# A decoder-style block in fp32 on one core: the even layer's third stream started three rounds later, and latent attention's preparation folded from 22 rounds into 13

## Chip, cores and metric

One core of one Trainium2 chip runs the whole program in one launch. The metric is the device time of that launch in microseconds. The engines are TensorE (PE in the profile, with PEld for its weight loads), VectorE (DVE), ScalarE (ACT), GpSimd (POOL) and SyncE (SP), which only issues loads.

## The reference, cut to what matters

The input is a sequence of 512 tokens by 1024 features in fp32. A first block is followed by a second one of two layers. The change lies in the mixer of the second block's layer 0, the even layer, which joins four heads of differential attention and four heads of latent attention:

```python
proj = h @ w_in                                       # aq, ak, av, cq, ckv, kr
# differential attention, head hd (4 of them), two softmaxes over the same values
p = probs(q1b, k1) - lam * probs(q2b, k2)
o_a = _rms(p @ va, g_sub) * (1.0 - lambda_init)
# latent attention, 4 heads
q = _heads(_rms(cq, g_cq) @ w_uq, MLA_HEADS)          # 256 -> 4 x (128 + 64)
q_nope, q_rope = q[..., :128], _rope(q[..., 128:], pos)
kv = _heads(_rms(ckv, g_ckv) @ w_ukv, MLA_HEADS)      # 128 -> 4 x (128 + 128)
k_nope, vb, k_rope = kv[..., :128], kv[..., 128:], _rope(kr, pos)
sc = (q_nope @ k_nope.T + q_rope @ k_rope.T) * MLA_SCALE
o_b = softmax(where(mask, sc, -inf)) @ vb
return concat([o_a, o_b]) @ w_out
```

## The kernel before

Activations lie as 128 features by 512 tokens. A product with a weight (`dense`, L152 for each matmul) is made in three passes of a split number: the weight's rounded part times the rounded activation, the same times the activation's rest, and the weight's rest times the rounded activation. With 1024 input features that is 8 x 3 = 24 matmuls of 128x512. Each weight unit (128x1024) is loaded into one of four `raw` buffers, rounded by ACT into one of three `wr` buffers (L165, `weight_hi`, two units ahead) and its rest is made by DVE (L171, `weight_lo`, one unit ahead).

`even_layer` weaves three streams. `weave` asks each stream in turn for its next piece of program, up to that stream's next `yield`. One turn of all streams is called a round here. It runs once for each engine with the same rounds, so the order of the instructions on PE, DVE and ACT is fixed when the program is built. Each engine works through its own queue in order, and waits on semaphores count finished instructions of the other engines.

- Stream A holds `mla()`, the preparation of latent attention, then `head(0)` and `head(1)` of latent attention. `mla_tensor`, `mla_vector` and `mla_scalar` write: `kr` (unit 15) with the statistics of two norms, its rotation, units 12 and 13 (`low`, the cq part) with the norm MQ, unit 14 with the norm MK, six products `uq` of 6 matmuls each, two rotations `qrp`, and per head `ukn`, `ukv` (3 matmuls each) and four transposes. On DVE eight multiplications of X by a gain (`scale_vector`, L1530) lie between the `uq`.
- Stream B holds `diff(0)`, `diff(2)` and latent `head(2)`.
- Stream C holds `diff(1)`, `diff(3)` and latent `head(3)`.

`diff` has three products q, k, v of 24 matmuls (one round each), then six steps, then two rounds for its norm (11 rounds). In step i PE makes the scores of query block i (`db_k,db_q` in stream B, `dc_k,dc_q` in C; 128 (i+1) keys, both softmaxes), the products with the values for block i-2, and the transposes of block i-1. DVE normalizes block i-1 (L1604 to L1610) and then finds the maxima of block i (L380). ACT takes the exponentials of block i (L1645) and copies the transposed block i-1 (L1654). In the last step DVE copies the head's output (L1620). A latent head has six rounds of the same kind, with one softmax.

PSUM has 8 banks. Three hold outputs of the streams, and everything else in this layer takes the next of banks 0 to 4 in turn (`K.ring(*range(5))`). PE may write a bank only when its last user has been read, so PE also waits for the exponentials of older scores.

## Time and profile before

| | us |
|---|---|
| median of 3 runs | 2167.02 (2165.88 to 2173.46) |
| profiled execution, its own time | 2172.61 |
| its span | 2171.4 |
| PE busy | 2030.9 (94%) |
| DVE busy | 1088.7 (50%) |
| ACT busy | 873.4 (40%) |
| chain that ended last, share of PE | 85% |

The span is what the trace covers, and lies 1.2 us under that execution's own time. The even layer runs from about 540 us to about 740 us of the span. PE's busy time counts a matmul that runs at the lower clock as busy, so time is lost in two ways: PE idle, and PE busy at half its clock.

### The profile page before, as it was taken

What the parts mean: (1) busy time and instruction counts of PE and PEld (TensorE: products, weight loads), DVE (VectorE), ACT (ScalarE), POOL (GpSimd) and SP (SyncE); (2) the same over time, 40 slices, a digit from 0 to 9 for tenths busy, and PEclk for the clock granted to TensorE, in tenths of its full rate; (3) what the DMA queues carried; (4) which work ended last, traced back from release to release, by engine and by line L of the source; (5) the groups of instructions that cost most, each with busy time, mean ns of one, the idle gap of its engine ahead of it and who ended that gap; (6) DMA issues with size and microseconds to landing.
All of it is one profiled execution on the core that took longest, in us unless ns stands there. A gap on an engine that the chain in (4) does not pass through costs nothing.

```text
span 2171.4 us, 28244 instructions
## 1 busy us (share of the span) xinstructions
PE 2030.9 (94%) x11400; PEld 1613.2 (74%) x11400; DVE 1088.7 (50%) x1929; ACT 873.4 (40%) x1567; POOL 27.3 (1%) x68
## 2 busy tenths in 40 slices
PE   6898888889989999999999999999899999999997
PEld 5765666777766679878888887667478978888886
DVE  5666468737465454354334354444355445343444
ACT  5325443244345444343223243566644344232332
POOL 0000000000000000000000000011000000000000
PEclk9989899999999999999999999999999999999999
DMA  5210011012211123122222222111023212222221
GB/s 200 88 49 21 20 59 49 3 60 101 88 49 49 39 97 127 68 88 97 90 104 89 98 95 88 59 49 49 30 97 113 102 59 97 97 97 97 97 97 69
DMA packets 52050, 169.63 MB, mean 78 GB/s; under 512 B 5776, under 2 KB 9424, under 8 KB 51920
## 3 DMA queue, kind: packets, MB, share of 16 engines
q1 hardware_dynamic: 51920, 167.82, 22.1%
q8 instruction: 92, 1.51, 0.3%
q14 instruction: 38, 0.31, 0.0%
HBM read 165.70 MB, written 2.10 MB: 77 GB/s over the span
## 4 chain that ended last, share of the span: by engine, by line
PE 85%; DVE 9%; ACT 4%; issue 1%; DMA 0%; POOL 0%; SPq 0%; DVEq 0%; ACTq 0%
PE ps L152 83%; PE ps L157 3%; DVE ps L380 1%; DVE wr L171 1%; DVE X L1530 0%; DVE lo L218 0%; DMA cst<-d_cst 0%; DVE macc L233 0%; DVE ra_S L769 0%; DVE rc_S L769 0%; DVE rb_S L769 0%; DVE ra_Z L789 0%; ACT sa_sp L2103 0%; DVE x_acc L233 0%; ACT wr L165 0%
## 5 line engine op out<-in xcount | busy, mean ns | idle before, releaser
L152 PE MATMUL ps<-hi,wr 128*128 128x512 f32 (+1 forms) x4616 | 1406.9, 385 | 50.1 <-DVE wr L171 34.2
L152 PEld LDWEIGHTS ps<-hi,wr 128*128 128x128 f32 x4616 | 861.9, 190 | 230.2 <-DVE wr L171 25.7
L152 PE MATMUL ps<-lo,wr 128*128 128x512 f32 (+1 forms) x2308 | 879.9, 381 | 0.0
L152 PEld LDWEIGHTS ps<-lo,wr 128*128 128x128 f32 x2308 | 439.6, 190 | 84.1 <-issue 3.9
L165 ACT ACTIVATE wr<-raw 128x1024 fp32r<-128x1024 f32 x293 | 307.6, 1052 | 349.6 <-PE ps L152 349.6
L171 DVE TENSOR_TENSOR wr<-raw,wr 128x1024 fp32r<-128x1024 f32 x293 | 356.7, 1217 | 4.3 <-ACT wr L165 2.3
L1457 DVE TENSOR_TENSOR X<-X,ps 128x512 f32<-128x512 f32 x96 | 66.0, 688 | 238.3 <-PE ps L152 238.3
L1986 ACT ACTIVATE mlp<-mlp 128x512 f32<-128x512 f32 x64 | 40.4, 632 | 207.8 <-DVE mlp L1969 207.8
L1969 DVE SCALAR_TENSOR_TENSOR mlp<-ps,R 128x512 f32<-128x512 f32 x64 | 44.3, 692 | 113.2 <-PE ps L152 106.2
L213 ACT ACTIVATE hi<-X,pv 128x512 fp32r<-128x512 f32 x48 | 34.7, 722 | 138.2 <-DVE X L1457 136.2
L1972 DVE TENSOR_TENSOR lo<-mlp,hi 128x512 fp32r<-128x512 f32 x64 | 44.3, 693 | 87.8 <-ACT hi L1990 87.8
L218 DVE SCALAR_TENSOR_TENSOR lo<-X,pv,hi 128x512 fp32r<-128x512 f32 x48 | 36.0, 751 | 40.7 <-ACT hi L213 40.7
L226 ACT ACTIVATE sq<-X 128x512 f32<-128x512 f32 x49 | 30.3, 618 | 28.9 <-DVE X L1457 28.9
L1990 ACT ACTIVATE hi<-mlp 128x512 fp32r<-128x512 f32 x64 | 40.4, 632 | 2.7 <-ACT mlp L1986 0.4
L426 ACT ACTIVATE x_pr<-ps,st 128x256 f32<-128x256 f32 x32 | 15.2, 475 | 61.8 <-DVE st L412 61.8
L233 DVE TENSOR_TENSOR acc<-acc,sq 128x512 f32<-128x512 f32 x50 | 34.6, 693 | 10.0 <-ACT sq L226 5.6
L274 DVE SCALAR_TENSOR_TENSOR Y<-ps,R 128x512 f32<-128x512 f32 x16 | 11.1, 692 | 55.2 <-PE ps L152 47.9
L152 PE MATMUL ps<-x_pt,vt 128*128 128x128 f32 x256 | 34.3, 277 | 2.6 <-ACT x_pt L437 2.6
L152 PEld LDWEIGHTS ps<-x_pt,vt 128*128 128x128 f32 x256 | 32.3, 191 | 5.2 <-ACT x_pt L437 4.3
L152 PE MATMUL ps<-sb_sp,cst 128*128 128x128 f32 (+3 forms) x84 | 26.8, 455 | 7.5 <-POOL sb_sp L2125 7.5
L152 PE MATMUL ps<-sa_sp,cst 128*128 128x128 f32 (+3 forms) x84 | 26.2, 450 | 7.0 <-POOL sa_sp L2125 7.0
L152 PE MATMUL ps<-kt,Y 128*128 128x256 f32 x128 | 32.6, 379 | 0.0
(696 smaller groups left out, 1877.4 us busy)
## 6 DMA issues: line engine op xcount, KB each, us to landing
raw<-d_w SPq DMA_DIRECT2D x128, 512.0 KB, 3.4
raw<-d_wkv SPq DMA_DIRECT2D x32, 512.0 KB, 3.5
raw<-d_w_in SPq DMA_DIRECT2D x30, 512.0 KB, 3.5
raw<-d_sb_w_in SPq DMA_DIRECT2D x24, 512.0 KB, 3.4
raw<-d_ev_w_in SPq DMA_DIRECT2D x16, 512.0 KB, 3.4
raw<-d_wq SPq DMA_DIRECT2D x16, 512.0 KB, 3.5
raw<-d_wo SPq DMA_DIRECT2D x16, 512.0 KB, 3.4
X<-d_xT SPq DMA_DIRECT2D x16, 256.0 KB, 5.1
```

The source lines that it names most:

```text
L152: return pe.matmul(out, lhsT, rhs, start=start, stop=stop, skip_group_check=True)
L157: return pe.transpose(out, in_, M.C("ident")[0:n, 0:n])
L165: a.activation(M.wr[u % 3][:, 0:1024], M.raw[u % 4], ACT.Copy).then_inc(*K.tell("act", "hi", u))
L171: v.tensor_tensor(w[:, 1024:2048], M.raw[u % 4], w[:, 0:1024].bitcast(F32), ALU.subtract).then_inc(*K.tell("dve", "lo", u))
L213: a.activation(hi, src, ACT.Copy, scale=gcol).then_inc(*K.tell("act", *name, "hi", i))
L218: v.scalar_tensor_tensor(out=lo, in0=src, scalar=gcol, in1=hi.bitcast(F32), op0=ALU.mult, op1=ALU.subtract).then_inc(*K.tell("dve", *name, ...
L233: v.tensor_tensor(acc, acc, tmp[i % 2], ALU.add).then_inc(*K.tell("dve", *name, "sum", i))
L1457: v.tensor_tensor(M.X[u], M.X[u], K.bank(*key, u), ALU.add).then_inc(*K.tell("dve", *key, u, frees=(*key, u)))
L1969: v.scalar_tensor_tensor(out=t, in0=K.bank(*key), scalar=0.0, in1=M.R, op0=ALU.max, op1=ALU.mult).then_inc(*K.tell("dve", *key, frees=key))
L1972: v.tensor_tensor(lo[u], t, hi[u].bitcast(F32), ALU.subtract).then_inc(*K.tell("dve", "h", n, q, "lo", u))
L1986: a.activation(t, t, ACT.Square).then_inc(*K.tell("act", *key, "sq"))
L1990: a.activation(hi[u], t, ACT.Copy).then_inc(*K.tell("act", "h", n, q, "hi", u))
```

## The change

The three generators of the preparation merge neighbouring rounds: the rotation of `kr` with units 12 and 13; the statistics of MQ with unit 14; the six `uq` in pairs; both `qrp` rotations in one round; and in the last part the transposes of head h-1 share a round with `ukn` and `ukv` of head h. That makes 13 rounds of 22. Stream C gets `idle(3)` in front. Nothing is computed otherwise. What stands in the rounds (B and C name the step of `diff` or of a latent head):

| round | A before | B, C before | A now | B now | C now |
|---|---|---|---|---|---|
| 1 | kr | q | kr | q | - |
| 2 | kr rotated | k | rotated, 12, 13 | k | - |
| 3 | 12, 13 | v | MQ, 14 | v | - |
| 4 | MQ | step 0 | MK | step 0 | q |
| 5 | 14 | 1 | uq 0, 1 | 1 | k |
| 6 | MK | 2 | uq 2, 3 | 2 | v |
| 7 | uq 0 | 3 | uq 4, 5 | 3 | step 0 |
| 8 | uq 1 | 4 | both qrp | 4 | 1 |
| 9 | uq 2 | 5 | ukv 0 | 5 | 2 |
| 10 to 11 | uq 3, 4 | norm | ukv 1, 2 | norm | 3, 4 |
| 12 to 13 | uq 5, qrp 0 | q, k | ukv 3, end | q, k | 5, norm |
| 14 to 19 | qrp 1, ukv 0, 1, 2 | v, 0 to 4 | head 0 | v, 0 to 4 | norm, q, k, v, 0, 1 |
| 20 to 22 | ukv 2, 3 | 5, norm | head 1 | 5, norm | 2 to 4 |
| 23 to 25 | head 0 | head 2, head 3 | head 1 | head 2 | 5, norm |
| 26 to 28 | head 0 | head 2, head 3 | none | head 2 | head 3 |
| 29 to 31 | head 1 | none | none | none | head 3 |
| 32 to 34 | head 1 | none | none | none | none |

```diff
--- before.py
+++ after.py
@@ -1676,12 +1676,10 @@
     between_tensor(K, M, pe)
     yield
     rope_tensor(K, M, pe, ("kr",), "rot_m", s.kr, K.done("dve", "kr"))
-    yield
     for u in (12, 13):
         dense(K, M, pe, ("low", u), "ev_w_in", u, hi, lo)
     yield
     stats_tensor(K, M, pe, MQ, M.acc, last=1)
-    yield
     dense(K, M, pe, ("low", 14), "ev_w_in", 14, hi, lo)
     yield
     stats_tensor(K, M, pe, MK, M.acc, last=0)
@@ -1694,23 +1692,27 @@
             pe.wait_ge(*K.done("dve", *MQ, "lo", 1))
         unit = dense(K, M, pe, ("uq", m), "uq", m // 4, q_hi, q_lo, nk=2, wk=m % 4 * 2,
                      same=unit if m % 4 else None, last=m in (3, 5))
-        yield
+        if m % 2:
+            yield
     for z in range(2):
         rope_tensor(K, M, pe, ("qrp", z), "rot_m", s.qrp[z], K.done("act", "uq", 4 + z))
-        yield
+    yield
     unit = None
-    for h in range(4):
-        if h == 0:
-            pe.wait_ge(*K.done("dve", *MK, "lo", 0))
-        unit = dense(K, M, pe, ("ukn", h), "ukv", 0, k_hi, k_lo, nk=1, wk=h, same=unit, last=False)
-        dense(K, M, pe, ("ukv", h), "ukv", 0, k_hi, k_lo, nk=1, wk=4 + h, same=unit, last=h == 3)
-        yield
-        b = K.take("ukv", h, "t")
-        pe.wait_ge(*K.clear("ukv", h, "t"))
-        pe.wait_ge(*K.done("act", "ukv", h))
-        for j in range(4):
-            done = tr(pe, M, b[:, j * 128:j * 128 + 128], s.pr[h % 2][:, j * 128:j * 128 + 128])
-        done.then_inc(*K.tell("pe", "ukv", h, "t"))
+    for step in range(5):
+        h = step - 1
+        if h >= 0:
+            b = K.take("ukv", h, "t")
+            pe.wait_ge(*K.clear("ukv", h, "t"))
+            pe.wait_ge(*K.done("act", "ukv", h))
+            for j in range(4):
+                done = tr(pe, M, b[:, j * 128:j * 128 + 128], s.pr[h % 2][:, j * 128:j * 128 + 128])
+            done.then_inc(*K.tell("pe", "ukv", h, "t"))
+        h = step
+        if h < 4:
+            if h == 0:
+                pe.wait_ge(*K.done("dve", *MK, "lo", 0))
+            unit = dense(K, M, pe, ("ukn", h), "ukv", 0, k_hi, k_lo, nk=1, wk=h, same=unit, last=False)
+            dense(K, M, pe, ("ukv", h), "ukv", 0, k_hi, k_lo, nk=1, wk=4 + h, same=unit, last=h == 3)
         yield
 
 
@@ -1731,13 +1733,11 @@
     yield
     v.wait_ge(*K.landed("mcs", 2))
     rope_vector(K, v, ("kr",), s.kr, s.kr, s.cos, s.sin, s.pr[0])
-    yield
     for n, u in enumerate((12, 13)):
         project(K, M, v, ("low", u), s.kn[n])
         add_square(K, v, MQ, n, M.acc, M.sq)
     yield
     low_vector(K, M, v, MQ, 2, "g_cq", s.kn[0:2], M.hi[0][0:2], M.lo[0][0:2])
-    yield
     project(K, M, v, ("low", 14), s.kn[2])
     yield
     low_vector(K, M, v, MK, 1, "g_ckv", s.kn[2:3], M.hi[0][2:3], M.lo[0][2:3])
@@ -1747,14 +1747,13 @@
             weight_lo(K, M, v)
         for i in range(m * ND // 6, (m + 1) * ND // 6):
             scale_vector(K, M, v, FIN, "norm_final_g", i, M.between.R)
-        yield
+        if m % 2:
+            yield
     for z in range(2):
         rope_vector(K, v, ("qrp", z), s.qrp[z], s.qrp[z], s.cos, s.sin, s.pr[z], K.done("act", "uq", 4 + z))
-        yield
-    for h in range(4):
-        if h == 0:
-            weight_lo(K, M, v)
-        yield
+    yield
+    weight_lo(K, M, v)
+    for _ in range(5):
         yield
 
 
@@ -1770,14 +1769,12 @@
     weight_hi(K, M, a)
     factors_scalar(K, M, a)
     yield
-    yield
     for n, u in enumerate((12, 13)):
         weight_hi(K, M, a)
         a.wait_ge(*K.done("dve", "low", u))
         square(K, a, MQ, n, s.kn[n], M.acc, M.sq)
     yield
     low_scalar(K, M, a, MQ, 2, 256, s.kn[0:2], M.hi[0][0:2])
-    yield
     weight_hi(K, M, a)
     a.wait_ge(*K.done("dve", "low", 14))
     square(K, a, MK, 0, s.kn[2], M.acc, M.sq)
@@ -1790,22 +1787,25 @@
         a.wait_ge(*K.done("pe", "uq", m))
         dst = M.Y[4 + m] if m < 4 else s.qrp[m - 4]
         a.activation(dst, K.bank("uq", m), ACT.Copy).then_inc(*K.tell("act", "uq", m, frees=("uq", m)))
-        yield
-    for z in range(2):
-        yield
-    for h in range(4):
-        if h == 0:
-            weight_hi(K, M, a)
-        a.wait_ge(*K.done("pe", "ukn", h))
-        if h == 0:
-            a.wait_ge(*K.done("dve", "qrp", 1, "rope"))
-        a.activation(s.kn[h], K.bank("ukn", h), ACT.Copy).then_inc(*K.tell("act", "ukn", h, frees=("ukn", h)))
-        a.wait_ge(*K.done("pe", "ukv", h))
-        a.activation(s.pr[h % 2], K.bank("ukv", h), ACT.Copy).then_inc(*K.tell("act", "ukv", h, frees=("ukv", h)))
-        yield
-        a.wait_ge(*K.done("pe", "ukv", h, "t"))
-        a.activation(s.vn[h], K.bank("ukv", h, "t"), ACT.Copy).then_inc(
-            *K.tell("act", "ukv", h, "t", frees=("ukv", h, "t")))
+        if m % 2:
+            yield
+    yield
+    for step in range(5):
+        h = step - 1
+        if h >= 0:
+            a.wait_ge(*K.done("pe", "ukv", h, "t"))
+            a.activation(s.vn[h], K.bank("ukv", h, "t"), ACT.Copy).then_inc(
+                *K.tell("act", "ukv", h, "t", frees=("ukv", h, "t")))
+        h = step
+        if h < 4:
+            if h == 0:
+                weight_hi(K, M, a)
+                a.wait_ge(*K.done("dve", "qrp", 1, "rope"))
+            a.wait_ge(*K.done("pe", "ukn", h))
+            a.activation(s.kn[h], K.bank("ukn", h), ACT.Copy).then_inc(*K.tell("act", "ukn", h, frees=("ukn", h)))
+            a.wait_ge(*K.done("pe", "ukv", h))
+            a.activation(s.pr[h % 2], K.bank("ukv", h), ACT.Copy).then_inc(
+                *K.tell("act", "ukv", h, frees=("ukv", h)))
         yield
 
 
@@ -1841,7 +1841,7 @@
 def even_layer(M, mla, head, diff):
     A, B, C = M.even.lanes
     weave(chain(mla(), head(0, A), head(1, A)), chain(diff(0, B), diff(2, B), head(2, B)),
-          chain(diff(1, C), diff(3, C), head(3, C)))
+          chain(idle(3), diff(1, C), diff(3, C), head(3, C)))
```

First place, PE where the scores of the first two differential heads begin (round 4 before). `acc,cst` is the column sum for a norm, `cst,db_pt` the transposes of the values of stream B, `dc` the same of stream C. Before:

```order
L152 MATMUL ps<-acc,cst 128x512
L157 MATMUL ps<-cst,db_pt_312 128x128 x4
L152 MATMUL ps<-db_k,db_q 128x128 x2
L157 MATMUL ps<-cst,dc_pt_320 128x128 x4
L152 MATMUL ps<-dc_k,dc_q 128x128 x2
L152 MATMUL ps<-hi_0_73,wr 128x512
```

In the changed kernel stream C comes to this point three rounds later, in round 7 and 8, with both rotations `mla_qr` behind it:

```order
L157 MATMUL ps<-cst,dc_pt_320 128x128 x4
L152 MATMUL ps<-dc_k,dc_q 128x128 x2
L152 MATMUL ps<-mla_qr_301,cst 128x512
L152 MATMUL ps<-mla_qr_302,cst 128x512
L152 MATMUL ps<-db_pt_311,db_v 128x128 x3
L157 MATMUL ps<-cst,db_pr_310 128x128 x4
L152 MATMUL ps<-dc_k,dc_q 128x256 x2
L157 MATMUL ps<-cst,dc_pr_317 128x128
```

What moved: behind the scores of stream C there is no product of 24 matmuls any more, but the two rotations and the fourth step of stream B.

Second place, DVE at those rotations (L1110, L1111, L1114 are one rotation, L171 a weight's rest, L274 and L277 read a product out of PSUM). Before, in rounds 12 to 14:

```order
L274 SCALAR_TENSOR_TENSOR dc_q<-ps,R 128x512
L1110 TENSOR_TENSOR mla_qr_301<-mla_qr_301,mla_cos 128x512
L1111 TENSOR_TENSOR mla_pr_303<-ps,mla_sin 128x512
L1114 TENSOR_TENSOR mla_qr_301<-mla_qr_301,mla_pr_303 128x512
L171 TENSOR_TENSOR wr<-raw,wr 128x1024
L277 TENSOR_TENSOR db_k<-ps,R 128x512
L171 TENSOR_TENSOR wr<-raw,wr 128x1024
L277 TENSOR_TENSOR dc_k<-ps,R 128x512
L1110 TENSOR_TENSOR mla_qr_302<-mla_qr_302,mla_cos 128x512
```

In the changed kernel, in round 8:

```order
L1110 TENSOR_TENSOR mla_qr_301<-mla_qr_301,mla_cos 128x512
L1111 TENSOR_TENSOR mla_pr_303<-ps,mla_sin 128x512
L1114 TENSOR_TENSOR mla_qr_301<-mla_qr_301,mla_pr_303 128x512
L1110 TENSOR_TENSOR mla_qr_302<-mla_qr_302,mla_cos 128x512
L1111 TENSOR_TENSOR mla_pr_304<-ps,mla_sin 128x512
L1114 TENSOR_TENSOR mla_qr_302<-mla_qr_302,mla_pr_304 128x512
L1604 RECIPROCAL st<-st 128x2
L1606 TENSOR_TENSOR st<-st,omm 128x1
L1607 TENSOR_SCALAR db_pr_310<-db_pr_310,st 128x512
L1610 SCALAR_TENSOR_TENSOR db_pr_310<-db_p_308,st,db_pr_310 128x512
```

What moved: both rotations now stand in one piece, directly ahead of the normalization of stream B's last block.

Third place, DVE in round 20, where a copy of a head's output (L1620, its output `Y_59`) meets the steps of stream C. In the changed kernel:

```order
L380 ISA ps,st<-ps,cmask 128x128
L380 ISA st 128x1
L1620 COPY Y_59<-ps 128x512
L1604 RECIPROCAL st<-st 128x2
L1606 TENSOR_TENSOR st<-st,omm 128x1
L1607 TENSOR_SCALAR dc_pr_318<-dc_pr_318,st 128x256
L1610 SCALAR_TENSOR_TENSOR dc_pr_318<-dc_p_316,st,dc_pr_318 128x256
```

Before, both streams reach this copy in the same round, with nothing of a softmax behind it. What moved: the copy, which waits for the last product of stream B with its values, now stands ahead of the normalization of stream C's block 1.

## Rows read from the trace of the kernel before

**Rows 1.** Stretches of the even layer: start:end, length, busy us (instructions), granted clock

```profile
core 0: us, PE busy (x) PEld busy (x) DVE busy (x) ACT busy (x) POOL busy (x), PEclk, DMA share, GB/s
540.00:588.00 48.00, 47.28 (x203) 37.82 (x202) 21.31 (x26) 12.21 (x15) 0.00 (x0) 1.00 0.28 98
588.00:603.00 15.00, 12.37 (x47) 9.10 (x46) 5.66 (x14) 6.00 (x15) 0.00 (x0) 0.77 0.11 38
603.00:628.00 25.00, 19.49 (x86) 11.16 (x85) 20.39 (x64) 14.38 (x39) 0.00 (x0) 0.86 0.06 22
628.00:671.00 43.00, 43.00 (x191) 34.45 (x190) 21.19 (x27) 13.52 (x18) 0.00 (x0) 1.00 0.25 86
671.00:699.00 28.00, 26.03 (x141) 17.42 (x141) 19.36 (x68) 20.87 (x57) 0.00 (x0) 1.00 0.05 20
699.00:727.00 28.00, 28.00 (x144) 17.46 (x143) 12.99 (x50) 15.03 (x43) 0.00 (x0) 1.00 0.01 1
727.00:739.00 12.00, 9.84 (x47) 5.59 (x46) 4.34 (x16) 4.59 (x14) 0.00 (x0) 1.00 0.00 0
739.00:748.00 9.00, 7.11 (x19) 5.67 (x20) 6.04 (x9) 5.60 (x10) 0.00 (x0) 0.62 0.00 0
```

**Rows 2.** Timeline of PE, 588 to 635 us: start, us, instruction [idle before <-releaser]

```profile
594.03 0.79 PE L152 MATMUL ps<-dc_k,dc_q 64*128 64x128 f32 x2 [2.18 <-ACT db_v L294]
595.27 0.79 PE L152 MATMUL ps<-hi,wr 128*128 128x512 f32 x1 [0.46 <-ACT db_pr L1645]
...
613.48 0.41 PE L157 MATMUL ps<-cst,db_pr 128*128 128x128 f32 x2 [2.64 <-DVE db_pr L1610]
```

**Rows 3.** Timeline of DVE: ends of two dense products, an output's copy, a rotation

```profile
603.36 0.69 DVE L277 TENSOR_TENSOR mla_kn<-ps,R 128x512 f32<-128x512 f32 x1 [6.71 <-PE ps L152]
...
630.04 0.69 DVE L1620 COPY Y<-ps 128x512 f32<-128x512 f32 x1 [1.76 <-PE ps L152]
...
642.24 0.69 DVE L274 SCALAR_TENSOR_TENSOR db_q<-ps,R 128x512 f32<-128x512 f32 x1 [3.23 <-PE ps L152]
...
647.68 0.69 DVE L274 SCALAR_TENSOR_TENSOR dc_q<-ps,R 128x512 f32<-128x512 f32 x1 [3.62 <-PE ps L152]
648.60 0.69 DVE L1110 TENSOR_TENSOR mla_qr<-mla_qr,mla_cos 128x512 f32<-128x512 f32 x1 [0.22 <-PE ps L152]
...
650.53 1.22 DVE L171 TENSOR_TENSOR wr<-raw,wr 128x1024 fp32r<-128x1024 f32 x1
```

**Rows 4.** Timeline of DVE, first instruction of each piece of a differential step

```profile
603.97 0.16 DVE L1604 RECIPROCAL st<-st 128x2 f32<-128x2 f32 x1
...
604.82 0.42 DVE L380 CUSTOM_DVE_ANT_0 ps<-ps,dist 128x256 f32<-128x256 f32 x1
...
617.62 0.74 DVE L1530 SCALAR_TENSOR_TENSOR X<-X,pv,r 128x512 f32<-128x512 f32 x1
618.28 0.16 DVE L1604 RECIPROCAL st<-st 128x2 f32<-128x2 f32 x1
...
619.53 0.69 DVE L380 CUSTOM_DVE_ANT_0 ps<-ps,dist 128x512 f32<-128x512 f32 x1
...
620.78 0.16 DVE L1604 RECIPROCAL st<-st 128x2 f32<-128x2 f32 x1
...
623.97 0.15 DVE L1604 RECIPROCAL st<-st 128x2 f32<-128x2 f32 x1
...
625.42 0.16 DVE L1604 RECIPROCAL st<-st 128x2 f32<-128x2 f32 x1
```

**Rows 5.** Timeline of ACT, one exponential of a 128x512 block

```profile
621.01 0.69 ACT L1645 ACTIVATE db_pr<-ps,st 128x512 f32<-128x512 f32 x1 [1.37 <-DVE st L1604]
```

**Rows 6.** Timeline of PE at the layer's end

```profile
735.59 0.93 PE L152 MATMUL ps<-mla_cos,mla_vn 128*128 128x128 f32 x6 [1.07 <-ACT mla_cos L437]
...
737.71 1.16 PE L152 MATMUL ps<-mla_sin,mla_vn 128*128 128x128 f32 x8 [0.75 <-ACT mla_sin L437]
...
740.89 0.77 PE L152 MATMUL ps<-hi,wr 128*128 128x512 f32 x1 [2.02 <-DVE lo L1438]
```

## The prediction

> **What bounds the kernel now.** The page comes first: PE is busy for 94% of the span and holds 85% of the chain that ended last, so time is lost only where PE waits or where its clock is low. The change touches the even layer alone, so the second view is the table of stretches from 540 to 748 us [rows 1]. The length of a stretch less PE's busy time is idle: 0.72, 2.63, 5.51, 0.00, 1.97, 0.00, 2.16 and 1.89 us, 14.9 us in all. The granted clock has two levels, 2.4 and 1.2 GHz, so a mean of 0.77 over 15 us is 2 x 0.23 x 15 = 6.9 us at the lower one. By the same sum it is 7.0 us between 603 and 628 and 6.8 us between 739 and 748. Everywhere else in the layer the clock is full.
>
> What does the low clock cost? A dense product takes 647.68 - 642.24 = 5.44 us at the full clock [rows 3]. The one that starts at 595.27 [rows 2] is read at 603.36 [rows 3], 8.1 us later, so it cost 2.6 us. Between 603 and 628 PE is busy for 78% of the time, which makes 7.0 x 0.78 / 2 = 2.7 us. After 741 PE is busy throughout: 6.8 / 2 = 3.4 us. Together that is 8.7 us. The whole layer thus loses 14.9 + 8.7 = 23.6 us, 1.1% of the kernel, and this is what a new order of rounds can win at most.
>
> Third view, the timeline of PE, for what it waited for. Before 594.03 stands a wait of 2.18 us until ACT had copied `db_v`, and 0.46 us follow. Before 613.48 stand 2.64 us until DVE had normalized a block [rows 2]. Both lie beside the norms MQ and MK: the chain of a norm goes from PE over ACT and DVE and back over ACT to DVE, and the softmax steps of both streams stand behind it in the same queues. At the end of the layer PE waits 1.07, 0.75 and 2.02 us for the last head's exponential, transposed block and split output [rows 6].
>
> **The change part by part.** PE's work is the same, instruction for instruction. Only idle time and time at the low clock change.
>
> *Rounds 1 to 3.* Only one product stands behind `kr` instead of two, but `kr`'s rotation and unit 12 follow, and the weight's rest for the second product, which PE waited for before (0.72 us [rows 1]), is then covered by the rotation's product. The norm MQ now has unit 14 (5.44 us) over it. Its DVE pieces stand ahead of the rest of stream B's v weight, which I work out to be about 0.4 us late. Idle: 0.4.
>
> *Rounds 4 to 6.* MK and step 0 lie over stream C's q product, and steps 1 and 2 over its k and v: 5.44 us of PE work in each round, where before rounds 4 and 6 had none. The waits of [rows 2] go. What stays are the transposes of blocks 0 and 1, which wait until DVE has done a weight's rest, two or three L1530 and block i-1. An L1530 takes 618.28 - 617.62 = 0.66 us [rows 4]. I count 0.6 + 0.1 us, and 0.4 us for a bank that an ACT copy frees late. Idle: 1.1.
>
> *Rounds 7 to 11* have no dense product. The DVE prices, from start to start, are: block 0 normalized 604.82 - 603.97 = 0.85; block 2 619.53 - 618.28 = 1.25, its maxima of block 3 another 620.78 - 619.53 = 1.25; block 3 625.42 - 623.97 = 1.45 [rows 4]; one rotation 650.53 - 648.60 = 1.93 [rows 3].
> Round 7: PE has two `uq` (12 of the 24 matmuls, 2.7 us), scores of block 3 (1.1 us, an estimate from PE's rate in the same fp32 form) and values (0.5 us), 4.3 us. DVE has reading v (0.6), a weight's rest (1.1), three L1530 (2.0) and block 2 (1.25), 5.0 us. With hand-over times PE waits 0.9 us. Then stream C's second score bank is the one of stream B's block 3, so PE waits for maxima (1.25) and one exponential (0.69 [rows 5]), 1.0 us more than it has work for.
> Round 8: PE has two rotations (1.7 us) and one product with values (0.7 us), then transposes of block 3. DVE must first do two rotations, 3.86 us, and block 3, 1.45 us, and can begin only when PE's first rotation product is done. From there PE has 1.6 us of work against 5.3 us: 3.7 to 3.9 us of waiting, and 0.4 us before it for the bank of the last score. Before, each rotation lay beside dense products, and cost nothing.
> Round 9: a weight's rest, the output copy (0.6 us, after the product with values it waits for) and block 1 stand before stream C's transposes: 1.0 us. Rounds 10 and 11: banks and block 3 of stream C, 1.2 us.
> Sum: 0.9 + 1.0 + 0.4 + 3.9 + 1.0 + 1.2 = 8.4 us idle.
>
> *Rounds 12 to 17* carry six dense products, one each: 0.3 us. *Rounds 18 to 22* have none, and the streams stand three rounds apart: in round 18 stream C's first scores wait for the bank of stream B's block 3 as in round 7 (1.0 us); in 19 and 20 block 3 and the output copy (0.69 us [rows 3], itself waiting for PE) stand ahead of stream C's normalization (0.6 and 0.9 us); with the maxima of head 1, 1.5 us in rounds 21 and 22. Sum 4.0 us, where the same steps idle for 1.97 us before [rows 1]. *Rounds 23 to 28*: 0.3 us.
>
> *Rounds 29 to 31.* Head 3 ends alone, as head 1 does now. Its last three steps have nothing beside them in either kernel. The waits of [rows 6] stay, 3.84 us. Only head 1's first three rounds alone disappear, and they idle for little: 2.16 - 1.07 - 0.75 = 0.34 us.
>
> *Sum of idle.* 0.4 + 1.1 + 8.4 + 0.3 + 4.0 + 0.3 + 3.8 = 18.3 us against 14.9 us: 3.4 us more.
>
> *The clock.* Its first fall before, at 594 us, comes after 2.64 us of idle within six. The wait of round 8 is of that size, so I take one such fall, 2.6 us, in place of the two stretches with 2.6 + 2.7 us. The last fall stays at 3.4 us. That is 2.7 us less. The Trainium skill, "TensorE: Matmul & The Clock Gate", section "A second HAM failure mode: psum-queue depth-cycling", says that PE's short idles between groups of matmuls, as it goes round the PSUM banks, are enough to swing its clock between the two levels. By that rule rounds 7 to 11, which wait on banks and on DVE again and again, would fall more than once, as 603 to 628 does here [rows 1]; the trace agrees in that stretch, and not between 671 and 699, where PE idles 1.97 us in 28 and the clock stays full.
>
> *Net.* +3.4 - 2.7 = +0.7 us on a profiled span of 2171.4 us and its own time of 2172.61 us. That execution is 5.6 us above the median of the runs shown, 2167.02 us, so I carry the difference over: 2167.7, say 2168 us. The work won is real (the norm waits), and it is given back on DVE.
>
> **The rivals.**
> *Faster: the queues slip past each other.* If stream C's three late rounds let DVE run ahead, the hand-made waits of rounds 7 to 11 and 18 to 22 (12.4 us) are half as long, and the clock stays full but for the end. For it: between 699 and 727 us three streams side by side leave PE no idle at all. Against it: there DVE has 13.0 us of work in 28, while rounds 7 to 11 have, by the prices above, about 22 us on DVE against about 20 on PE. Then 6.2 us of idle and the 2.6 us fall go: 2168 - 8.8 = 2159 us.
> *Slower: the pile of round 8 takes the clock down for several rounds.* The place is the transposes of stream B's block 3, behind both rotations. If the clock stays low through rounds 8 to 11, PE's 15 us of work there takes twice as long, less what hides in the waits (about 5 us): +10 us less the 2.6 already counted, about +7.5. The same in rounds 18 to 22, at a third of the size, adds 2: 2177 us. It decides from some 4 us of waiting in one piece on: the largest before, 2.64 us in one piece, was followed by 7 us low at most. By the skill's rule named above this case is the likelier the more banks PE waits for; the rows show it only for 603 to 628.
> *No effect of its own: the losses stay where they are, only with other names*, which is my forecast.
>
> **How the numbers follow.** My case 0.56 (2162 to 2173, from half of the 12.4 us of new waits being off by 5), faster rival 0.23, slower rival 0.21. 0.5% is 10.8 us, about what a measurement of this kernel can tell from no change. Faster than 2156.2 needs the faster rival and 3 us more, also from the end: 0.13. Slower than 2177.9 is the upper half of the slower rival: 0.12. Within: 0.75. The range, 2156 to 2178, reaches over both rivals' centres. The bounds are the 23.6 us that could be won and some 12 us of the slower rival.
>
> **What the profile of the changed kernel would show.** Right: from 588 us on no wait above 1 us for `db_v` or beside the norms; one wait of 3 to 4 us before the transposes of `db_pr`, released by L1610, with L1110 to L1114 twice before it on DVE; waits of 0.5 to 1 us on `dc_pr` near the layer's last quarter; the same three waits at the end, and a low clock behind them. The layer ends within 5 us of 740.9. Wrong: no such wait in round 8 (then DVE was ahead), a clock below 0.7 over 15 us or more, or an end without the fall of the clock.

## The result and the profile after

The changed kernel takes 2173.22 us (median of 20 runs, 2168.98 to 2176.36); the kernel before took 2167.61 us (20 runs, 2164.38 to 2173.52). The ratio is 1.0023, 95% interval 1.0014 to 1.0031: 3.0 to 6.7 us slower, about 5.0. That is clear of noise, and inside the 0.5% that I had called no change. A second series gave 1.0021 [1.0008, 1.0033].

The profiled execution has a span of 2169.1 us and its own time of 2170.41 us, which is *below* before's profiled 2172.61 us. So one pair of executions says the opposite of the medians, and the first thing to read is where two executions of one program differ. I cut each span into three parts: up to the second norm's `facc,cst` product on PE, from there to PE's first product behind the layer, and the rest. The cuts are these rows of PE's timeline (start, us, instruction, [idle before <-releaser]). Before:

```profile
542.68 1.02 PE L152 MATMUL ps<-facc,cst 128*128 128x512 f32 x2
```

The layer's end before is the last of [rows 6]. After, first and last:

```profile
537.54 1.02 PE L152 MATMUL ps<-facc,cst 128*128 128x512 f32 x2
...
733.00 0.94 PE L152 MATMUL ps<-dc_pt,mla_vn 128*128 128x128 f32 x6 [1.07 <-ACT dc_pt L437]
735.12 1.16 PE L152 MATMUL ps<-dc_pt,mla_vn 128*128 128x128 f32 x8 [0.75 <-ACT dc_pt L437]
738.30 0.47 PE L152 MATMUL ps<-hi,wr 128*128 128x512 f32 x1 [2.02 <-DVE lo L1438]
```

The layer is 740.89 - 542.68 = 198.2 us before and 738.30 - 537.54 = 200.8 us after. Cut in the same way, every trace of this study, in us (the last column is the median of that kernel's runs, for the first two kernels of their first series of 20, and the ratio to the kernel before in the same series):

| kernel | ahead | layer | behind | median, ratio |
|---|---|---|---|---|
| before, three traces | 542.7, 538.9, 542.0 | 198.2, 198.3, 198.2 | 1430.5, 1431.1, 1427.4 | 2167.6 |
| changed, three traces | 537.5, 538.1, 542.4 | 200.8, 200.4, 200.6 | 1430.8, 1430.8, 1430.9 | 2173.2, 1.0023 |
| only the packing | 541.6 | 197.7 | 1430.6 | 2168.8, 1.000 |
| scale steps early | 538.4 | 198.0 | 1427.4 | 2168.0, 1.0002 |
| one rotation late | 542.1 | 198.2 | 1430.5 | 2169.9, 1.0007 |
| both rotations late | 536.8 | 194.6 | 1431.0 | 2164.3, 0.9983 |
| rotations late, scales early | 541.7 | 194.5 | 1430.4 | 2165.5, 0.9986 |
| rotations late, no distance | 542.5 | 193.8 | 1430.8 | 2163.9, 0.9983 |
| rotations late, distance 2 | 539.3 | 191.4 | 1427.5 | 2162.2, 0.9968 |
| both moves, distance 2 | 540.7 | 190.5 | 1430.8 | 2161.9, 0.9967 |

The layer repeats within 0.4 us. The parts ahead of it and behind it hold the same instructions in all kernels, and from one execution to the next the first moves by up to 6 us and the second by up to 3.7. So the layer column is read first, and a median of many runs second.

The stretches of [rows 1], in the changed kernel:

```profile
core 0: us, PE busy (x) PEld busy (x) DVE busy (x) ACT busy (x) POOL busy (x), PEclk, DMA share, GB/s
540.00:588.00 48.00, 47.12 (x205) 36.57 (x204) 27.26 (x43) 19.30 (x32) 0.00 (x0) 1.00 0.26 89
588.00:603.00 15.00, 14.91 (x67) 11.51 (x66) 7.56 (x16) 5.96 (x11) 0.00 (x0) 1.00 0.19 69
603.00:628.00 25.00, 18.95 (x76) 11.84 (x75) 16.19 (x46) 9.68 (x28) 0.00 (x0) 0.80 0.12 43
628.00:671.00 43.00, 41.14 (x194) 30.43 (x193) 18.43 (x45) 19.50 (x44) 0.00 (x0) 1.00 0.14 50
671.00:699.00 28.00, 25.62 (x135) 17.96 (x133) 15.88 (x54) 11.22 (x32) 0.00 (x0) 1.00 0.11 38
699.00:727.00 28.00, 25.57 (x128) 15.58 (x128) 14.80 (x50) 15.40 (x45) 0.00 (x0) 1.00 0.00 1
727.00:739.00 12.00, 8.16 (x40) 4.88 (x39) 4.60 (x13) 5.95 (x15) 0.00 (x0) 1.00 0.00 0
739.00:748.00 9.00, 9.00 (x35) 7.28 (x34) 6.08 (x10) 4.67 (x8) 0.00 (x0) 0.81 0.06 18
```

The layer from cut to cut, before and after:

```profile
542.68:740.89 198.21, 183.34 (x842) 131.16 (x840) 104.23 (x263) 88.38 (x201) 0.00 (x0) 0.96 0.15 51
537.54:738.30 200.76, 183.23 (x841) 129.85 (x840) 104.87 (x263) 87.63 (x201) 0.00 (x0) 0.97 0.15 50
```

PE has the same matmuls in both, so a difference in its busy time is read here as what the clock costs, and the rest is idle. Idle time grew from 14.87 to 17.53 us, and busy time is 0.11 us less.

588 to 603 us, which lost 2.63 us of idle and a fall of the clock before, loses nothing now. 603 to 628 idles for 6.05 us in place of 5.51, and has a clock of 0.80: 2 x 0.20 x 25 = 10.0 us at the lower level in place of 7.0. The two stretches from 671 to 727 us idle for 4.8 us in place of 1.97. What sits in 603 to 628 is the pile, on PE and then on DVE:

```profile
606.44 0.52 PE L157 MATMUL ps<-cst,db_pr 128*128 128x128 f32 x3 [0.83 <-DVE db_pr L1610]
...
608.53 0.48 PE L152 MATMUL ps<-dc_k,dc_q 64*128 64x128 f32 x2 [0.72 <-ACT db_pr L1645]
609.20 3.68 PE L152 MATMUL ps<-mla_qr,cst 128*128 128x512 f32 x4 [0.18 <-ACT db_p L1645]
...
617.03 1.09 PE L157 MATMUL ps<-cst,db_pr 128*128 128x128 f32 x4 [3.49 <-DVE st L1604]
...
625.48 0.41 PE L157 MATMUL ps<-cst,dc_pr 128*128 128x128 f32 x2 [0.66 <-DVE dc_pr L1610]
```

```profile
611.26 0.69 DVE L1110 TENSOR_TENSOR mla_qr<-mla_qr,mla_cos 128x512 f32<-128x512 f32 x1 [1.50 <-PE ps L152]
...
613.41 0.69 DVE L1110 TENSOR_TENSOR mla_qr<-mla_qr,mla_cos 128x512 f32<-128x512 f32 x1
...
615.35 0.16 DVE L1604 RECIPROCAL st<-st 128x2 f32<-128x2 f32 x1
...
616.14 0.75 DVE L1610 SCALAR_TENSOR_TENSOR db_pr<-db_p,st,db_pr 128x512 f32<-128x512 f32 x1
```

DVE has waited 1.50 us for PE's first rotation product, does both rotations from 611.26 to 615.35, normalizes block 3, and PE starts its transposes at 617.03, after 3.49 us. (The timeline names `st` L1604 as releaser; L1610 ends at the same moment, 616.14 + 0.75 us.) The transposes then last 1.09 us, where the same four take 0.63 us at the full clock in two kernels below: the clock is at its lower level. The stretches of the same trace, at the places where the clock changed:

```profile
609.34:612.75 3.41, 3.41 (x5) 1.34 (x6) 1.88 (x7) 1.37 (x6) 0.00 (x0) 0.50 0.00 0
612.75:616.17 3.42, 0.79 (x7) 0.60 (x5) 3.18 (x8) 0.00 (x0) 0.00 (x0) 1.00 0.00 0
616.17:622.99 6.82, 5.96 (x20) 4.43 (x21) 3.46 (x10) 3.27 (x9) 0.00 (x0) 0.50 0.09 22
```

It falls twice. The first time is ahead of the wait, for the 3.4 us of the rotation products: the four matmuls take 3.68 us, and 1.98 us at the full clock in a kernel below. The second time begins while PE still waits, at 616.17, and is twice as long. Half of PE's busy time at the low clock is (3.41 + 5.96) / 2 = 4.7 us. That is an estimate of the loss, and a rough one, since the transposes above grew by less than double.

### The profile page after: what moved, and what is told of

It is laid out like the page before. It is cut to its first block, busy times and chain, and to the rows that moved or that the text cites. A ratio compares the mean times of both kernels' runs of the same rounds, so it can differ in the third digit from the quotient of the medians.

```text
span 2169.1 us, 28244 instructions
## 1 busy us (share of the span) xinstructions
PE 2026.7 (93%) x11400; PEld 1608.4 (74%) x11400; DVE 1089.5 (50%) x1929; ACT 873.4 (40%) x1567; POOL 27.4 (1%) x68
## 4 chain that ended last, share of the span: by engine, by line
PE 85%; DVE 10%; ACT 3%; issue 1%; DMA 0%; POOL 0%; SPq 0%; DVEq 0%; ACTq 0%
PE ps L152 82%; PE ps L157 3%; DVE ps L380 1%; DVE wr L171 1%; DVE X L1530 0%; DMA cst<-d_cst 0%; DVE lo L218 0%; DVE macc L233 0%; DVE ra_S L769 0%; DVE rc_S L769 0%; DVE rb_S L769 0%; DVE x_acc L233 0%; DVE nsa_pra L401 0%; ACT sa_sp L2103 0%; ACT L248 0%
## 5 line engine op out<-in xcount | busy, mean ns | idle before, releaser
L171 DVE TENSOR_TENSOR wr<-raw,wr 128x1024 fp32r<-128x1024 f32 x293 | 356.9, 1218 | 4.3 <-ACT wr L165 2.3
L274 DVE SCALAR_TENSOR_TENSOR Y<-ps,R 128x512 f32<-128x512 f32 x16 | 11.1, 692 | 53.3 <-PE ps L152 46.1
```

The costliest lines, as they stand in the source:

```text
L171: v.tensor_tensor(w[:, 1024:2048], M.raw[u % 4], w[:, 0:1024].bitcast(F32), ALU.subtract).then_inc(*K.tell("dve", "lo", u))
```

## The experiments

The theory on trial: the layer loses its time at the pile of round 8, where DVE does two rotations and block 3 with nothing for PE beside them, by the wait and by what it does to the clock. The rivals: the packing itself (any order of the preparation in 13 rounds), the eight L1530 steps of rounds 5 to 7, and the distance of three rounds. In the expectations these are the pile theory and, for the distance, the stagger theory. Every kernel below computes the whole reference.

**Only the packing.** The distance is taken out of the changed kernel:

```diff
-          chain(idle(3), diff(1, C), diff(3, C), head(3, C)))
+          chain(diff(1, C), diff(3, C), head(3, C)))
```

> The preparation in 13 rounds, stream C not delayed (28 rounds in all). If the pile of both rotations ahead of the normalizations in round 8 is what costs, it is here too, with two streams behind it: a wait of 3.5 us or more before the transposes of block 3, a low clock after it, and no gain over the kernel before (2168 to 2176 us). If the delay of stream C is what costs (its steps against the output copies of stream B in rounds 18 to 22), this kernel is faster than the kernel before by 3 to 8 us, since its last head has company to the end: the waits of 1.07 and 0.75 us at the end shrink.

2168.8 us, ratio 1.000 [0.999, 1.0009], layer 197.7 us against before's 198.2 and the changed kernel's 200.6. So the pile by itself, with its wait of 4.34 us, doesn't make the layer longer than before; the 2.4 us come with the distance. The norm's waits are back, and a pile stands at another place (PE's timeline):

```profile
599.01 0.79 PE L152 MATMUL ps<-dc_k,dc_q 64*128 64x128 f32 x2 [1.51 <-ACT db_v L294]
...
608.32 0.30 PE L157 MATMUL ps<-cst,dc_pr 128*128 128x128 f32 x1 [1.00 <-DVE dc_pr L1610]
...
629.91 1.09 PE L157 MATMUL ps<-cst,db_pr 128*128 128x128 f32 x4 [4.34 <-DVE st L1604]
...
739.38 0.47 PE L152 MATMUL ps<-hi,wr 128*128 128x512 f32 x1 [2.02 <-DVE lo L1438]
```

At the layer's end only 2.02 us stay: the 1.07 and 0.75 us of [rows 6] have another stream's work over them. The packing alone wins that and pays it back at its own pile. The other half, the distance alone with 22 rounds, wasn't tried.

**Both rotations moved beside a dense product.** Out of round 8, into round 13 with `df2`'s k product; the `ukv` rounds move up by one. ACT also loses a wait there: it no longer waits for the second rotation before its first copy of `ukn`. On PE (DVE and ACT follow):

```diff
         if m % 2:
             yield
-    for z in range(2):
-        rope_tensor(K, M, pe, ("qrp", z), "rot_m", s.qrp[z], K.done("act", "uq", 4 + z))
-    yield
     unit = None
...
             dense(K, M, pe, ("ukv", h), "ukv", 0, k_hi, k_lo, nk=1, wk=4 + h, same=unit, last=h == 3)
         yield
+    for z in range(2):
+        rope_tensor(K, M, pe, ("qrp", z), "rot_m", s.qrp[z], K.done("act", "uq", 4 + z))
+    yield
```

> The changed kernel with both rotations moved from round 8 to round 13, where a dense product of 24 matmuls lies beside them; the rounds of ukv move up by one. Pile theory: the wait of 3.49 us and the two low stretches of the clock after it (10.2 us low in the changed kernel's trace, about 4 us lost) go, 2173.2 - 3.5 - 3 = 2166 to 2168 us. Stagger theory: the waits only move to the next step of stream C, 2171 to 2174 us.

2164.34 us, ratio 0.9983 [0.9975, 0.9992]; layer 194.6 us, 6.1 us less than the changed kernel's first trace and 3.6 us less than before's. The time is 2 us under the 2166 to 2168 that the pile theory gave. PE waits 0.27 us at most right around block 3's transposes, and 603 to 628 us read:

```profile
603.00:628.00 25.00, 21.59 (x106) 14.26 (x105) 15.99 (x50) 16.68 (x42) 0.00 (x0) 0.93 0.13 43
```

2 x 0.07 x 25 = 3.5 us at the low clock in place of 10.0, and 2.6 us less idle. Over the whole layer idle time is 14.3 us in place of 17.5, and busy time 180.3 in place of 183.2: the gain is 3.2 us of waiting and 2.9 us of clock. In their new place the rotations have 1.88 us of PE's rotation products and the 24 matmuls of `df2` beside them and cost no wait.

**Only one rotation moved.** The first stays in round 8, the second goes to round 13, all rounds stay where they are:

```diff
-    for z in range(2):
-        rope_tensor(K, M, pe, ("qrp", z), "rot_m", s.qrp[z], K.done("act", "uq", 4 + z))
+    rope_tensor(K, M, pe, ("qrp", 0), "rot_m", s.qrp[0], K.done("act", "uq", 4))
     yield
...
+        if step == 4:
+            rope_tensor(K, M, pe, ("qrp", 1), "rot_m", s.qrp[1], K.done("act", "uq", 5))
         yield
```

> The changed kernel with only one of the two rotations left in round 8 (the second moves to round 13, beside df2's k product), nothing else moved: half the pile. Theory of the pile, by size: the wait before block 3's transposes falls from 3.49 us by one rotation, 1.93 us, to about 1.6 us, and the clock stays low for 3.4 us in place of 10.2 us between 603 and 628, which gives back some 2 us more; the layer, 200.8 us in the changed kernel, takes 196 to 198 us, and the time is 2167 to 2170 us, half way to the kernel with both rotations late. Rival, threshold: only a wait as long as the changed kernel's takes the clock down; then half a move brings nearly all, 2164 to 2166 us. Rival, block 3 itself is what is late: the wait stays above 3 us and the time at 2172 us.

2169.85 us, ratio 1.0007 [0.9993, 1.002]; layer 198.2 us. PE's wait and the clock:

```profile
619.53 0.63 PE L157 MATMUL ps<-cst,db_pr 128*128 128x128 f32 x4 [2.56 <-DVE st L1604]
```

```profile
614.20:617.60 3.40, 2.77 (x8) 1.54 (x7) 1.89 (x5) 1.07 (x5) 0.00 (x0) 0.63 0.00 0
617.60:621.00 3.40, 1.47 (x8) 0.92 (x8) 2.49 (x9) 0.60 (x1) 0.00 (x0) 0.87 0.00 0
621.00:624.40 3.40, 3.40 (x15) 2.67 (x14) 1.95 (x5) 2.06 (x7) 0.00 (x0) 0.63 0.11 14
```

The wait fell by 0.93 us and not by a rotation's 1.93: with one rotation PE also has one product less to do, so it begins to wait earlier. The clock still falls twice, but the second fall lasts 3.4 us instead of 6.8. Against the changed kernel's first trace the layer has 1.1 us less idle and 1.5 us less busy, so about as much comes from the clock as from the wait. The rival of a threshold gave 2164 to 2166 us and is out: half the pile brought 2.5 of the 6.1 us, without moving any round. My 1.6 us for the wait was wrong by 1 us, the low clock lasts 6.8 us and not the 3.4 that I expected, and the layer lies 0.2 us over the range that I gave.

**Only the scale steps moved** from rounds 5 to 7 to rounds 3 and 4, four each; the rotations stay in round 8. On DVE:

```diff
     project(K, M, v, ("low", 14), s.kn[2])
+    for i in range(0, 4):
+        scale_vector(K, M, v, FIN, "norm_final_g", i, M.between.R)
     yield
     low_vector(K, M, v, MK, 1, "g_ckv", s.kn[2:3], M.hi[0][2:3], M.lo[0][2:3])
+    for i in range(4, ND):
+        scale_vector(K, M, v, FIN, "norm_final_g", i, M.between.R)
     yield
...
-        for i in range(m * ND // 6, (m + 1) * ND // 6):
-            scale_vector(K, M, v, FIN, "norm_final_g", i, M.between.R)
```

> The changed kernel with the eight multiplications of X by its gain (L1530) moved from rounds 5 to 7 to rounds 3 and 4. Pile theory: they cause only the waits of 0.84 and 0.83 us before the transposes of blocks 0 and 2, so 1 to 2 us less than the changed kernel, with the 3.5 us of round 8 still there: 2171 to 2173 us. If DVE's sum over rounds 5 to 9 is what counts and not the place of a piece, 5 us of DVE work less there shortens the wait of round 8 too: 2166 to 2169 us.

2167.97 us, ratio 1.0002 [0.9994, 1.0011]; layer 198.0 us, 2.8 us less than the changed kernel. This is more than the 1 to 2 us that the pile's theory gave, and the time lies in the range of the other theory. But that theory had the wait at block 3 shorter, and it grew:

```profile
609.55 1.98 PE L152 MATMUL ps<-mla_qr,cst 128*128 128x512 f32 x4 [0.18 <-ACT db_p L1645]
...
616.54 1.09 PE L157 MATMUL ps<-cst,db_pr 128*128 128x128 f32 x4 [4.34 <-DVE st L1604]
```

```profile
605.00:617.00 12.00, 6.91 (x34) 4.13 (x34) 8.69 (x24) 3.61 (x11) 0.00 (x0) 0.98 0.13 44
617.00:620.40 3.40, 3.40 (x13) 2.14 (x13) 1.79 (x6) 1.18 (x4) 0.00 (x0) 0.58 0.02 5
```

The gain is the clock: the layer idles for 17.9 us (17.5 in the changed kernel), and PE is busy for 180.1 us in place of 183.2. The fall ahead of the pile is gone, so the rotation products take 1.98 us in place of 3.68 and PE reaches the same wait earlier, and the fall behind it lasts 3.4 us. Of the falls, then, the first hangs on the scale steps in rounds 5 to 7, not on the pile: at distance 3 it stands in all five traces that have these steps there, and in neither of the two that don't. With them gone PE's wait of 0.83 us is gone too, and the 0.72 us is 0.57. With the rotations late and the scale steps in place the waits are 0.83 and 0.71 us, and this fall is there from 608.45 us.

**Both moves.** The two edits together:

> Both moves together: rotations in round 13, multiplications in rounds 3 and 4. Pile theory: 2164 to 2167 us, at or a little below the kernel before, since the waits beside the norms stay gone and rounds 18 to 22 and the end stay as they are. Stagger theory: no better than 2170 us.

2165.54 us, 0.9986 [0.9976, 0.9996]; layer 194.5 us, as with the rotations alone. The moves don't add up. The two waits of 0.83 us go, but the four scale steps of round 3 stand ahead of a weight's rest, and PE has a wait that the changed kernel doesn't have:

```profile
586.35 0.47 PE L152 MATMUL ps<-hi,wr 128*128 128x512 f32 x1 [1.23 <-DVE wr L171]
```

Block 3's transposes wait for 0.90 us again, and the layer idles for 14.8 us, 0.5 more than with the rotations alone.

**The distance, with the rotations late.** One number is changed, to 0 and to 2:

```diff
-          chain(idle(3), diff(1, C), diff(3, C), head(3, C)))
+          chain(idle(2), diff(1, C), diff(3, C), head(3, C)))
```

> Rotations in round 13 and stream C not delayed. Pile theory: against the kernel with 13 rounds and no delay, the wait of 4.34 us and the low stretch of 3.4 us after it go, so about 6 us less than that kernel: 2161 to 2164 us, ahead of all so far. Stagger theory (the delay is what the rotations' move needed): no faster than the same move with the delay, 2164 to 2167 us.

> Rotations in round 13 and stream C two rounds behind in place of three. If the waits of rounds 18 to 22 and the two at the end come from the distance of three rounds, one of them is shorter here: 2162 to 2166 us. If any distance costs the same, 2164 to 2166 us as with three.

No distance: 2163.94 us, 0.9983 [0.9971, 0.9995], layer 193.8 us. The 4.34 us of the kernel with only the packing are 1.27 here, but the layer is 3.9 us shorter than there and not 6, and the time is that of the same move at distance 3 (2164.34), as the stagger theory had it. Distance 2: 2162.21 us, 0.9968 [0.9957, 0.9979], layer 191.4 us, 3.3 us less than at distance 3. It also has the lower part behind in its one trace, so the layer is what the comparison rests on. 2.3 of the 3.3 us are idle time (12.0 us for 14.3), most of it behind 670 us: without the three waits at the end, which stay as they are, PE's waits there add up to 3.3 us in place of 4.8. Around block 3 of this kernel PE's timeline reads:

```profile
611.54 0.30 PE L157 MATMUL ps<-cst,dc_pr 128*128 128x128 f32 x1 [0.97 <-ACT db_pr L1645]
...
614.85 0.63 PE L157 MATMUL ps<-cst,db_pr 128*128 128x128 f32 x4 [0.34 <-DVE st L1604]
```

Its transposes take 0.63 us, and from 600 to 630 us its granted clock is 1.00. Distances 1 and 4 weren't tried.

Four layers now stand in a square, and it says what the changed kernel suffers from:

| layer, us | no distance | distance 3 |
|---|---|---|
| rotations in round 8 | 197.7 | 200.6 |
| rotations in round 13 | 193.8 | 194.6 |

The pile costs 3.9 us without the distance and 6.0 with it. The distance costs 2.9 us with the pile and 0.8 without it. Neither is the cause alone: the distance turned a small gain of the packing into a loss, and it did so mostly by way of the pile.

**Both moves at distance 2**, the last try at a better kernel:

> Rotations late, the eight scale steps early, and stream C two rounds behind in place of three. Theory: the two moves share one gain and the early scale steps cost a wait of 1.2 us for a weight's rest, so this takes as long as the kernel with the rotations late and a distance of two (2162.2 us), 2161 to 2165 us, layer 191 to 193 us. Rival, the moves add up once the distance is two: 2157 to 2160 us, layer under 190 us.

2161.87 us, 0.9967 [0.9952, 0.9981], layer 190.5 us: 0.9 us less in the layer, nothing that the medians can tell. A wait of 1.43 us for a weight's rest stands at 590.89 us, as in the kernel with both moves above. These two kernels beat the kernel before by 0.3%, 7 us.

**The same kernels again.** The kernel before against itself, the changed kernel again, and a third trace of each:

> The kernel before against itself: ratio 0.999 to 1.001, which says how small a difference these runs can tell. The layer takes 196 to 200 us by the same two rows as 198.2 us in the first trace; a spread of more than 2 us between the two traces would say that single traces cannot carry a difference of 2.5 us.

> The changed kernel once more, unchanged, for a second trace and a second ratio. If the 5 us are the layer's own, the layer (from the statistics of the second norm to the first product behind it) again takes 2 to 3 us more than in the kernel before, and the rest of the 5 us is to be found in where the clock falls; ratio 1.0015 to 1.003. If the first ratio was a matter of how runs fell, it comes out nearer 1.000.

> The changed kernel once more, for a third trace. The layer took 200.8 and 200.4 us in the first two and lies 2.2 to 2.5 us over before's, while the medians differ by some 5 us. Theory that the layer holds all of the difference when the clock falls as it mostly does: this trace has a longer layer, 202 to 204 us, with more time at the low clock. Rival, the layer is the same each time (200.4 to 200.8 us) and the rest of the difference lies ahead of it or behind it: the layer takes 200.8 us again, and the stretches around it are longer than before's.

> The kernel before once more, for a third trace beside the changed kernel's. Layer 198.2 us again by both theories; what lies ahead of it took 542.7 and 538.9 us in two traces with the same instructions, so a third says how far this part moves by itself: 537 to 543 us.

Before against itself: 1.0001 [0.999, 1.0013]. The changed kernel: 1.0021 [1.0008, 1.0033]. The layers are in the table above; they are the same in all three traces of each kernel, so nothing is left for the theory that the layer is longer in most executions than in the profiled one. What differs is ahead (537.5 to 542.7 us) and behind. Behind the layer stand two values only, 1427.4 to 1427.5 us in three of the fourteen traces and 1430.4 to 1431.1 us in eleven. They part mainly in one stretch, where the same instructions run with and without time at the low clock; before's first trace and its third:

```profile
1560.00:1580.00 20.00, 12.74 (x40) 5.67 (x38) 5.03 (x11) 9.92 (x18) 1.18 (x4) 0.83 0.00 1
```

```profile
1560.00:1580.00 20.00, 11.14 (x46) 5.06 (x43) 6.98 (x15) 13.60 (x25) 1.17 (x4) 1.00 0.00 1
```

0.17 x 2 x 20 = 6.8 us at the low clock, 3.4 us of work. The changed kernel has this low stretch in all three of its traces, and the kernel before in two. Three traces of each can't show how often it comes, but every execution also has its mean granted clock on record. Over all 33 runs of the changed kernel it is 0.97082 on average, and over 99 runs of the kernel before 0.97206. That is 2 x 0.00124 x 2168 = 5.4 us more at the lower level, while in the layer and the fall at its end the changed kernel has less of it than before (13.7 us for 20.5 in the first traces, 17.1 in the others). So more of the low clock lies outside the layer. Half of it, 2.7 us, is the most that it can cost, and that is the size of what the layer doesn't hold. Why the clock is lower there stays open.

## Why the prediction was right, and where not

The forecast was 2168 us, no change. Measured are +5.0 us by the ratio, of which the layer holds +2.4 (200.6 against 198.2, means of three traces). "No change" held, and so did where PE waits. The net of +0.7 us was too low, and the sum behind it was right in its idle time only: a band of 0.5% is wide enough to hold a gain of the clock that didn't come. The median, 2173.2 us, lies just past the end of the 2162 to 2173 us that I gave to my own case.

*The idle time, step by step.* Rounds 1 to 6: forecast 0.4 + 1.1, measured 48 - 47.12 = 0.88 and 15 - 14.91 = 0.09. The waits for `db_v` and for the norms are gone, as forecast. Rounds 7 to 11: forecast 8.4, measured 0.83 + 0.72 + 0.18 + 3.49 + 0.66 and, up to 635 us, another 0.17 + 0.29 + 0.36: 6.7 us. The wait of round 8 was forecast at 3.7 to 3.9 and is 3.49 to 3.77 in the traces of this kernel, with L1110 to L1114 twice before it. The round before it was priced too high, 1.9 for 1.5, and the rounds after it at 2.2 for 1.5. Rounds 12 to 17: forecast 0.3, measured 0.78 + 0.34 = 1.1. Rounds 18 to 22: forecast 4.0, measured on PE's timeline:

```profile
685.74 0.66 PE L157 MATMUL ps<-cst,mla_pr 128*128 128x128 f32 x4 [0.71 <-DVE mla_pr L401]
689.85 0.49 PE L152 MATMUL ps<-dc_k,dc_q 64*128 64x128 f32 x2 [0.57 <-ACT db_pr L1645]
692.53 0.63 PE L157 MATMUL ps<-cst,db_pr 128*128 128x128 f32 x4 [0.43 <-ACT Y L1837]
697.70 0.41 PE L157 MATMUL ps<-cst,dc_pr 128*128 128x128 f32 x2 [0.66 <-DVE dc_pr L1610]
705.05 0.94 PE L152 MATMUL ps<-dc_pt,dc_v 128*128 128x128 f32 x6 [0.35 <-ACT dc_pt L1654]
706.92 0.63 PE L157 MATMUL ps<-cst,dc_pr 128*128 128x128 f32 x4 [0.94 <-DVE st L393]
```

3.7 us. Rounds 23 to 28: forecast 0.3, measured 0.71 + 0.43 = 1.1. The end: the same three waits, 3.84 us. All stretches together idle for 0.88 + 0.09 + 6.05 + 1.86 + 2.38 + 2.43 + 3.84 = 17.5 us; forecast were 18.3, 14.9 before. That the sum is so near is in part luck: rounds 7 to 11 were priced 1.7 us too high, and the two groups at 0.3 us together 1.6 us too low.

*The clock: the step that was mis-sized.* I took one fall of 2.6 us after round 8 in place of two stretches with 2.6 + 2.7 us, and booked 2.7 us as a gain. There are two falls again, 3.4 us ahead of the wait and 6.8 us behind it. PE's busy time in the layer says what that is worth: 183.34 us before and 183.23 after, so the gain is 0.1 us (0.5 by the means of three traces, 183.4 and 182.9). The last kernel tried, whose layer has no low clock at all, is busy for 178.4 us:

```profile
540.72:731.23 190.51, 178.37 (x841) 127.59 (x840) 104.85 (x263) 87.21 (x201) 0.00 (x0) 1.00 0.16 53
```

By this estimate, which compares different orders of the rounds, the clock cost 5.0 us in the layer before, near the 5.3 that I read, and costs 4.9 in the changed kernel where I took 2.6. Half of PE's busy time in the low stretches gives 6.3 and 4.7 us instead, a gain of 1.6. Either way the 2.7 us are not there, and only the first way adds up to the layer's time. Idle +2.7 and clock -0.1 make the +2.6 us of the layer in the first traces. The forecast had +3.4 and -2.7.

The last fall was forecast to stay at 3.4 us of lost work. In the changed kernel the clock is low for 3.4 us in all three traces, from 739.05 us in the first, and costs 1.7. But it is as short in the second and third trace of the kernel before, and 6.8 us only in the first. Its size there was read from one execution and is no property of the change.

*The rivals.* "The queues slip past each other" did not happen: the hand-made waits came nearly all. "The pile of round 8 takes the clock down for several rounds" is half right: the clock is low for 10 us in rounds 7 to 9, but in work that it slows by about 5 us, not by 10, and in rounds 18 to 22 it doesn't fall. The Trainium skill's rule in "TensorE: Matmul & The Clock Gate", section "A second HAM failure mode: psum-queue depth-cycling", by which PE's short idles between groups of matmuls swing the clock, fits the first fall from 603 to 628 us, which follows waits of 0.83 us on DVE and 0.72 us on a bank. The second follows 3.49 us in one piece, which is another case. And it does not fit from 671 to 727 us: PE idles there for 4.8 us in eight pieces, none above 0.94 us, and the clock stays at 1.00.

*Shown and not shown.* Shown: the two rotations in round 8 cost 6.1 us of the layer at a distance of three rounds (by moving them), about half of it by the clock; with one of them moved 2.4 us are won; the packing alone changes nothing that the times can tell; the distance of three rounds is worse than two by 3.3 us once the rotations are out of the way. Argued only: that the move of the `ukv` rounds by one, which came with both rotations, is worth nothing. Not shown: where and why the clock is low for the other 2.6 us of the difference.

## What to carry to other kernels

When rounds are packed, add up for each round what every engine has to do: a round that holds pieces of one engine alone makes the others wait (here PE 3.49 us for 5.6 us of DVE work), and here the cure was to put these pieces beside a dense product five rounds later. Where two parts of a change may act on each other, test both with and without the other: here the distance cost 2.9 us of the layer with the pile and 0.8 without it. A wait on the matmul engine is priced with the fall of its clock near it, and that part was about as large as the wait. Cut the span into parts that hold the same instructions before two single executions are compared: here the layer repeated within 0.4 us while the part ahead of it moved by up to 6.

## What the runs showed of the hardware that I had not expected

How long the clock stays low doesn't follow from the length of the wait alone: a wait of 4.34 us was followed by 3.4 us at the low level with the scale steps early, one of 3.49 us by 6.8 us in the changed kernel, where the clock had already been low once just before. It also fell with small waits only: with the rotations late none above 0.83 us stands near, and still it was low from 608.45 to 611.86 us:

```profile
609.00:612.40 3.40, 3.40 (x14) 2.84 (x13) 3.26 (x10) 3.01 (x8) 0.00 (x0) 0.58 0.39 131
```

And the same instructions in the same order ran with a fall or without one in different executions of one kernel (1560 to 1580 us above), which moved the time by 3.4 us.
